# Two units of the first layer worked chunk by chunk in one pass, and the order of the loads at the kernel's start

## What is computed

```
def reference(x, norm1_g, w_in, ...):
    h = x
    for l in range(DEPTH):
        h = h + hybrid_mixer(rmsnorm(h, norm1_g[l]), w_in[l], ...)
        h = h + conv_glu_ffn(rmsnorm(h, norm2_g[l]), w_up[l], ...)
    return rmsnorm(h, final_g)

def hybrid_mixer(xn, w_in, ...):
    u = xn @ w_in
    qa, ka, va, qb, kb, vb, qc, kc, vc, fc = jnp.split(u, offs, axis=-1)
    ...
    gates = jax.nn.sigmoid(xn @ w_gate + b_gate)
    merged = gates_a * (ya @ w_br_a) + gates_b * (yb @ w_br_b) + gates_c * (yc @ w_br_c)
    return merged @ w_out
```

## Time and profile before

| | us |
|---|---|
| median of 3 executions | 1451.21 |
| lowest and highest | 1450.91 and 1452.52 |
| the profiled execution, its time | 1451.6 |
| the profiled execution, its span on the core | 1449.8 |
| mean granted TensorE clock | 0.999 of full speed |

### The profile page before, as it was taken

The page is one execution under the profiler, slowest core; times in us unless marked ns, Lnnn a source line. Parts: engine busy times, 40 slices in busy tenths (PEclk is TensorE's granted clock), DMA queues, the critical chain, the costliest instruction groups (busy, mean ns, idle before and its releaser), DMA issues.

```text
span 1449.8 us, 20293 instructions
## 1 busy us (share of the span) xinstructions
PE 1434.9 (99%) x6949; PEld 1183.1 (82%) x6949; DVE 1086.4 (75%) x1836; ACT 731.3 (50%) x1259; POOL 40.0 (3%) x30
## 2 busy tenths in 40 slices
PE   9999999999999999999999999999999999999997
PEld 7888888888888888878877888888888888888886
DVE  7877667656688888897787776676557888888976
ACT  7645555434533433476675555544335343344665
POOL 0000000002100000000010000000021000000001
PEclk9999999999999999999999999999999999999999
DMA  6222222242454654465622222222434555555654
GB/s 251 88 73 89 77 70 73 78 140 101 146 192 171 217 191 171 181 227 161 208 88 87 76 86 74 73 73 81 135 101 149 208 179 193 206 177 191 209 167 145
DMA packets 54327, 203.07 MB, mean 140 GB/s; under 512 B 7008, under 2 KB 7136, under 8 KB 48368
## 3 DMA queue, kind: packets, MB, share of 16 engines
q1 hardware_dynamic: 47488, 156.87, 32.7%
q10 hardware_dynamic: 6768, 45.27, 8.2%
HBM read 176.89 MB, written 25.17 MB: 139 GB/s over the span
## 4 chain that ended last, share of the span: by engine, by line
PE 86%; DVE 7%; ACT 3%; DMA 2%; issue 1%; SPq 0%; ACTq 0%; DVEq 0%
PE dense L813 23%; PE dense L815 22%; PE dense L814 22%; PE turned L896 2%; PE dense L1061 1%; PE dense L1059 1%; PE dense L1060 1%; PE branch L923 1%; DMA raw<-in_w_last 1%; PE dense L828 1%; PE dense L830 1%; PE dense L829 1%; PE scores L1059 1%; PE scores L1061 1%; PE scores L1060 1%
## 5 line engine op out<-in xcount | busy, mean ns | idle before, releaser
L813 PE MATMUL dense<-hg,whi 128*128 128x512 f32 x1296 | 514.2, 397 | 0.8 <-DVE hg L1601 0.2
L815 PE MATMUL dense<-hg,wlo 128*128 128x512 f32 x1296 | 506.1, 391 | 0.0
L814 PE MATMUL dense<-hg,whi 128*128 128x512 f32 x1296 | 505.3, 390 | 0.0
L1161 ACT ACTIVATE whi<-raw 128x1024 fp32r<-128x1024 f32 (+1 forms) x209 | 214.3, 1026 | 393.2 <-PE dense L815 387.5
L813 PEld LDWEIGHTS dense<-hg,whi 128*128 128x128 f32 x1296 | 244.0, 188 | 54.7 <-DVE wlo L1574 3.6
L1574 DVE TENSOR_TENSOR wlo<-raw,whi 128x1024 fp32r<-128x1024 f32 (+1 forms) x209 | 246.7, 1181 | 54.6 <-ACT whi L1161 52.1
L815 PEld LDWEIGHTS dense<-hg,wlo 128*128 128x128 f32 x1296 | 243.3, 188 | 52.1
L814 PEld LDWEIGHTS dense<-hg,whi 128*128 128x128 f32 x1296 | 243.8, 188 | 47.3 <-issue 0.2
L813 PE MATMUL dense<-act,whi 128*128 128x512 f32 x256 | 101.6, 397 | 0.9 <-DVE wlo L1574 0.9
L815 PE MATMUL dense<-act,wlo 128*128 128x512 f32 x256 | 99.8, 390 | 0.0
L814 PE MATMUL dense<-act,whi 128*128 128x512 f32 x256 | 99.8, 390 | 0.0
(11 more groups left out here) (348 smaller groups left out, 2071.2 us busy)
## 6 DMA issues: line engine op xcount, KB each, us to landing
raw<-in_w_up SPq DMA_DIRECT2D x88, 512.0 KB, 3.6
raw<-in_w_gate SPq DMA_DIRECT2D x48, 512.0 KB, 3.5
probT<-in_w_last ACTq DMA_DIRECT2D x20, 1024.0 KB, 6.3
w_sums<-probT ACTq DMA_DIRECT2D x20, 1024.0 KB, 4.3
raw<-in_w_in SPq DMA_DIRECT2D x26, 512.0 KB, 4.0
raw<-w_sums SPq DMA_DIRECT2D x16, 768.0 KB, 5.0
raw<-in_w_out SPq DMA_DIRECT2D x16, 512.0 KB, 3.5
raw<-in_w_last SPq DMA_DIRECT2D x14, 512.0 KB, 4.9
```

What stands on the lines that cost most here:

```text
L813: mm(out, a, xhi, start=start, stop=False)
L814: mm(out, a, xlo, start=False, stop=False)
L815: return mm(out, b, xhi, start=False, stop=stop)
L1161: fn(whi[:, s, 0:cols], raw[:, r, 0:cols], ACT.Copy).then_inc(w_hi.sem, 1)
```

## The change

Units 0 and 1 of the first layer are worked in one pass by a new function `first_pair`: both on chunks 0 and 1 (unit 0 first, then unit 1), and from chunk 2 on unit 0 and unit 1 by turns for each chunk. Both use `first_mm`. SyncE loads unit 1's halves between the chunks of x. ScalarE rounds and VectorE splits them in between too, and ScalarE squares chunks 0 to 2 between its copies of x. Unit 3's load waits for the last chunk of x, and the constants and tables come behind unit 3's load.

```
@@ block.sync
             load_x(1)
+            load_second(0)
             load_x(3)
             sp.dma_start(raw[:, 0, SLOT // 2:SLOT], A["w_in"][0, 0, :, SLOT // 2:SLOT]).then_inc(raw_in[0], 16)
-            for c in range(4, C):
+            load_x(4)
+            load_second(1)
+            for c in range(5, C):
                 load_x(c)
...
-                    if (l, n) == (0, 1):
-                        load_second()
-                    elif n > 0:
+                    if (l, n) == (0, 3):
+                        sp.wait_ge(x_in_s[C - 1], 16)
+                    if n > 1 - l:
                         load_mixer(l, n)
-                    if l == 0 and n == 2:
+                    if l == 0 and n == 3:
                         sp.dma_start(consts[:, :], A["consts"]).then_inc(const_in, 16)
-                    if n == 2 - l:
+                    if n == 3 - 2 * l:
                         load_layer_head(l)
@@ block.tensor
+            def first_pair():
+                def step(n, c):
+                    pe.wait_ge(hg_hi.sem, hg_hi.at(0, c - C))
+                    return first_mm(bank[n][:, :], c * P, n, hg[:, 0, c, :], hg[:, 1, c, :], c == 0, c == C - 1, c)
+
+                pe.wait_ge(half_lo, 1)
+                step(0, 0)
+                step(0, 1)
+                pe.wait_ge(second_lo, 1)
+                step(1, 0)
+                step(1, 1)
+                for c in range(2, C):
+                    for n in range(2):
+                        if c == C // 2:
+                            pe.wait_ge(w_lo.sem, w_lo.at(0, n))
+                        last = step(n, c)
+                        if c == C - 1:
+                            last.then_inc(used.sem, 1)
...
             for l in range(L):
-                if l > 0:
+                if l == 0:
+                    first_pair()
+                else:
                     first_units(l)
-                for n in range(0 if l == 0 else 2, NMIX):
+                for n in range(2, NMIX):
@@ block.scalar
             for c in range(C):
                 first_hi(c)
+                if c == 1:
+                    first_whi(1, second_in, True, second_hi)
                 if c == 3:
-                    act.wait_ge(raw_in[0], 16)
-                    fn(whi[:, 0, SLOT // 2:SLOT], raw[:, 0, SLOT // 2:SLOT], ACT.Copy).then_inc(w_hi.sem, 1)
+                    first_whi(0, raw_in[0], False, w_hi.sem)
+                if c == 4:
+                    first_square(0)
+                    first_whi(1, raw_in[1], False, w_hi.sem)
+                if c in (5, 6):
+                    first_square(c - 4)
...
                     if l == 0 and n == 0:
-                        for c in range(C):
+                        for c in range(3, C):
                             first_square(c)
                             if c == 3:
                                 split_hi_mixer(l, 2)
@@ block.vector
             for c in range(C):
...
+                if c == 1:
+                    first_wlo(1, second_hi, 1, True, second_lo)
                 if c == 3:
...
+                    first_wlo(0, w_hi.sem, w_hi.at(0, 0), False, w_lo.sem)
+                if c == 4:
+                    first_wlo(1, w_hi.sem, w_hi.at(0, 1), False, w_lo.sem)
```

51 lines of the change are left out of this document (15 added, 36 removed).

## The result

The changed kernel takes **1454.65 us** (median of 15 executions, 1452.66 to 1455.44), the kernel before 1451.89 in the same comparison (15 executions, 1450.61 to 1452.80). The ratio is 1.0019, its 95% interval 1.0011 to 1.0027. So the change made the kernel 2.8 us slower, just under the 0.2% that the prediction called the same; the time lies 0.85 us above the end of its range. The direction of the forecast was right, the size was three times too small (+0.9). Two executions far outside all others are left out of what follows, except where all eleven of e7 are named: one of the kernel before of 5113.68 us, and one of e7 of 2414.61 us with a mean granted clock of 0.556.

The account below looks back on a forecast made before the run. TensorE, busy 1434.9 of 1449.8 us, bounds the kernel; the pair's 1.0 us gain is spent, the reciprocal and the sixth unit's start at 38.48 move by +0.9, giving 1452.1 us against a median of 1451.2, range 1450.2 to 1453.8.

Parts of the forecast that it names:

- the 0.2% that the prediction called the same: Whole kernel: a change within 0.2%, 2.9 us, can't be told from none; chance of this outcome 0.91.
- TensorE's pair: First two units on TensorE: waits inside chunks go, one of 0.85 comes, end at 17.9, 1.0 us earlier.
- ScalarE's and VectorE's queues: Start of kernel: ScalarE's last copy of x at 14.0 instead of 11.16, VectorE's first add at 15.6, 1.4 later.
- the rival in which the weights are in the way of x by a later landing: ScalarE's queue: a later half tile delays everything behind it, 0.8 us per place (1452.9, 1453.7); chance 0.22.
- the other rival: Start of kernel: the pair's 1.0 us gain is kept and the reciprocal follows, giving 1450.2; chance 0.15.
- SyncE's wait, constants and tables: SyncE's queue: loads put behind the last x chunk's arrival cost nothing, at most about 0.2 us.
- All three move by 1.4.: Fourth square, copy of the third unit's weights and VectorE's split of them each start 1.4 us later.
- this term (+0.4 to +1.7): Delay of TensorE's start of the sixth unit at 38.48: +0.9 us, bounds +0.4 to +1.7; chance 0.58.
- The clock.: Rival before the third unit: TensorE's clock falls in the new 1.3 us wait, costing 3.4 us (1455.5); chance 0.02.
- The base.: Kernel before: median 1451.2 of three runs, which differ by 1.6 us, more than the forecast term.
- the three signs: Proved wrong if last copy of x starts before 13, third unit doesn't wait, or sixth starts before 38.5.

Follow-up runs that it names:

- e7: e3 with the squares of chunks 0 to 2 put back behind ScalarE's copies of x; 1451.77 us, ratio 1.0000 to the kernel before.
- e6: Changed kernel without SyncE's wait for the last chunk of x, constants and tables back in their old place; 1454.10 us, ratio 1.0019.
- e3: Changed kernel with the first layer's third unit's weights in a pair of tiles of their own; 1451.93 us, ratio 1.0004 to the kernel before.
- e4: Kernel before, with TensorE waiting ahead of the third unit until VectorE has added the last square; 1454.01 us, ratio 1.0014.
- e1: The changed kernel itself, run once more beside the kernel before; 1454.19 us, ratio 1.0018.
- e5: Kernel before, with TensorE's wait in the second layer filled with 24 matmuls on zeros; 1451.17 us, ratio 0.9997.
- e8: Changed kernel with e3's tiles, three chunks of lead, third and fourth units' copies moved ahead, second layer's wait filled; 1450.77 us, ratio 0.9993 to the kernel before.
- e9: Changed kernel with all three waits, two at the start and one in the second layer, filled with matmuls on zeros; 1452.23 us, ratio 1.0002.
- e11: e7 plus three chunks of lead, fourth unit's copy between squares, sixth unit's split moved ahead, second layer's wait filled; 1450.23 us, ratio 0.9991 to the kernel before.

## Why the prediction missed

It named the right places. Point by point:

- *TensorE's pair*: a wait of 0.85 for the second unit's first half, none in the later chunks, end at 17.9. Measured: 0.80 by the matmuls (1.14 by the weight loads) at 8.36, none, last matmul at 17.78, which makes TensorE free at 18.0. Right.
- *ScalarE's and VectorE's queues*: last copy of x at 14.0, first add at 15.6. Measured 13.88 and 15.36. Right; e7 confirms that the squares ahead of it are 1.6 of it. The half tile of weights was there at 6.95, where ScalarE's copy of it starts, as forecast: the rival in which the weights are in the way of x by a later landing didn't happen. The gain that the other rival saw is there only without the squares and the tile (e7).
- *SyncE's wait, constants and tables*: nothing. e6: nothing. The rule of the Trainium skill that speaks against such a wait ("DMA: Bandwidth & Descriptors", section "Rules for kernel authors": issue early, wait late) found no cost here: with it the time is 1454.19 and 1454.65, without it 1454.10.
- *"All three move by 1.4."* **This step failed.** It followed the third unit's copy back along its own engine, from the square and the add ahead of it, and left out the other thing that the copy waits for: the tile that it writes. The pair moves the last use of the first unit's tile from before 13.4 to 17.5, so the copy moves by 2.13 and not by 1.4, the reciprocal by 1.53 and not by 0.9. The part that it did have was a little too large: the queue moved the copy by 1.15, and with 0.6 of slack in place of 0.5 that alone would have given about +0.55. The third unit's wait, said to be 1.3, measured 1.79. The bounds given for this term (+0.4 to +1.7) hold 1.52, but by their width, not by this mechanism. e3 is the proof: with a tile of its own the copy has no wait, and the sixth unit is 1.2 earlier, 1.0 of it by the tile.
- *The clock.* **The second step that failed**, and the one that put the time outside the range. The rival was there, priced at 3.4 us with a chance of 0.02, on the ground that the clock was still full over 1442 to 1447 while TensorE idled and that 1.3 us is far shorter. What the runs show: in all eight falls it comes behind the wait, not in it, and waits of 2.2 and 2.7 us between busy stretches bring it in part of the executions (e4, e1), while with waits of about 1 us at the start there is no extra group (e3). The kernel's end, where nothing follows, could not show that. The wait of 2.69 at 771.72 was in the trace of before, with a full clock behind it in that one execution, and the median of the kernel before held a part of its cost already (e5). The price was too high, too: it took 15 matmuls at the lower level, for which no row stood; the clock is back after 3.4 us, time for some 8 of them at 0.45, and one fall costs 1.25 us.
- *The base.* The prediction spoke of 1.6 us between executions as noise to be larger than the term. Most of it was no noise but this fall, present or absent: with it filled away, eleven executions differ by 0.9 (e5). And the three executions of before had a median of 1451.21, where the fifteen beside the changed kernel have 1451.89; 0.7 of the distance between 1452.1 and 1454.65 is the base.

In the sum: +0.9 was forecast; 1.06 to 1.5 of order and 1.0 to 1.7 of clock came. With the tile seen, the forecast would have been +1.5 and 1452.7, inside its own range, and the result still outside. None of the three signs by which the prediction wanted to be proved wrong came: the last copy of x was not before 13, the third unit waited, the sixth was not before 38.5. They watched the queue, not the tile or the clock.

## What to carry to other kernels

When two pieces of work are interleaved, each holds its buffers for as long as both take: for every buffer that is reused, look up who writes it next, and put that writer's wait at the new last use, beside its queue's. Read the time of each execution with its mean clock, and not only the median and one trace: groups of times a fixed step apart are an effect that comes and goes, and the one profiled execution may be without it. Where TensorE must wait some 2 us in a kernel that keeps it busy, try to fill the wait with harmless matmuls or to shorten it to 1; the fill cost nothing here and took 2.0 to 2.4 us off the changed kernel, and 0.7, less than the comparison can tell, off the kernel before.

## What was unexpected in the hardware

- The granted clock fell 0.6 us (e4) and about 1 us (e1) after TensorE had started work again, behind waits of 2.19 and 2.69 us, to 1.2 GHz, and was full again 3.4 us later; it cost 1.25 us (e1). All eight falls in the traces lasted 3.4 us.
- It doesn't come every time, with the same instructions and the same wait: behind the second layer's wait of 2.65 to 2.71 us seven of nine profiled executions have it, and by its times the changed kernel has none in 4 of 37, one in 18 and two in 15. What decides between executions stays open.
- Small matmuls on zeros were enough to prevent it: with 24 of them in the second layer's wait none of four profiled executions has it (e5, e8, e9, e11), the spread went from 2.7 to 0.9 us (e5), and with all waits filled it was 0.6 (e9).
